# Gate and up products of a two-block network by Strassen's scheme, with the weight sums on GpSimd

## What is computed

```python
D_FF = 2816
def swiglu(h, w_gate, w_up, w_down):      # h: 512 x 1024, w_gate, w_up: 1024 x 2816, w_down: 2816 x 1024
    return (jax.nn.silu(h @ w_gate) * (h @ w_up)) @ w_down
```

## Time and profile before

| | |
|---|---|
| median of 3 runs | 3660.88 us (3645.41 to 3666.68) |
| profiled execution | 3647.48 us, span 3645.7 us |
| TensorE busy | 3278.3 us (90%) |
| VectorE, ScalarE, GpSimd busy | 1494.4, 1061.4, 171.7 us |
| granted TensorE clock, mean | 0.948 |
| one gate and up stage of an FFN | 238.6 us |

### The profile page before, as it was taken

One profiled execution on the slowest core, in us unless ns is written; L12 is line 12 of the kernel. 1 busy time (PEld: TensorE's weight loads), 2 busy tenths in 40 slices (PEclk: granted clock), 3 DMA queues, 4 the chain that ended last, 5 costly groups with the idle time before them and its releaser, 6 DMA issues. The chain is left out here.

```text
span 3645.7 us, 53714 instructions
## 1 busy us (share of the span) xinstructions
PE 3278.3 (90%) x23844; PEld 2475.4 (68%) x23844; DVE 1494.4 (41%) x2122; ACT 1061.4 (29%) x1666; POOL 171.7 (5%) x167
## 2 busy tenths in 40 slices
PE   6988778887998875999998799999999998799999
PEld 5856667764443333887786478878887886478877
DVE  3356665556121115333434553334333334553333
ACT  3226433321100002222323642223222323652222
POOL 0002222131000000000000000000000000000000
PEclk8999888997999997999999799999999999799999
DMA  6140000013799995222221032223332131032221
GB/s 235 58 159 1 3 4 3 34 64 136 317 408 422 421 421 201 93 93 93 74 106 58 1 104 93 93 93 99 102 100 93 70 110 58 1 104 93 93 93 41
DMA packets 173986, 441.04 MB, mean 121 GB/s; under 512 B 5954, under 2 KB 97852, under 8 KB 149180
## 3 DMA queue, kind: packets, MB, share of 16 engines
q1 hardware_dynamic: 173756, 437.61, 32.4%
HBM read 435.49 MB, written 2.10 MB: 120 GB/s over the span
## 5 line engine op out<-in xcount | busy, mean ns | idle before, releaser
L338 PE MATMUL banks<-mix_r,ring_r 128*128 128x512 f32 x1680 | 660.2, 393 | 0.0
L338 PE MATMUL banks<-mix_r,ffn_r 128*128 128x512 f32 x1568 | 622.4, 397 | 0.0
L338 PE MATMUL banks<-h_r,ffn_r 128*128 128x512 f32 x1568 | 610.2, 389 | 0.0
L295 DVE TENSOR_TENSOR ring_r<-ring,ffn_r 128x2048 fp32r<-128x2048 f32 (+1 forms) x166 | 354.9, 2138 | 220.6 <-ACT ffn_r L292 220.3
L292 ACT ACTIVATE ffn_r<-ring 128x2048 fp32r<-128x2048 f32 (+1 forms) x166 | 297.5, 1792 | 449.8 <-PE banks L338 440.5
L338 PEld LDWEIGHTS banks<-mix_r,ring_r 128*128 128x128 f32 x1680 | 315.4, 188 | 78.0
L338 PEld LDWEIGHTS banks<-h_r,ffn_r 128*128 128x128 f32 x1568 | 294.3, 188 | 68.5
L338 PEld LDWEIGHTS banks<-mix_r,ffn_r 128*128 128x128 f32 x1568 | 294.3, 188 | 62.2
L2261 PE MATMUL banks<-ring,arena 128*64 128x512 f32 x1120 | 261.6, 609 | 43.1 <-DMA ring<-in_exp_w_gate 16.8
L2887 PE MATMUL banks<-ring_r,ffn_r 128*128 128x512 f32 x704 | 279.3, 397 | 0.0
L2886 PE MATMUL banks<-ffn_r 128*128 128x512 f32 x640 | 250.7, 392 | 4.7 <-DVE arena L2837 4.7
(11 more groups left out here) (451 smaller groups left out, 5169.9 us busy)
## 6 DMA issues: line engine op xcount, KB each, us to landing
ring<-in_exp_w_gate SPq DMA_DIRECT2D x31, 2048.0 KB, 17.6
ring<-in_w_ffn_gate SPq DMA_DIRECT2D x44, 1024.0 KB, 5.4
ring<-in_w_ffn_up SPq DMA_DIRECT2D x44, 1024.0 KB, 8.0
ring<-in_exp_w_down SPq DMA_DIRECT2D x20, 2048.0 KB, 17.7
ring<-in_w_ffn_down SPq DMA_DIRECT2D x20, 2048.0 KB, 7.8
ring<-in_exp_w_up SPq DMA_DIRECT2D x19, 2048.0 KB, 14.8
ring<-in_w_in SPq DMA_DIRECT2D x17, 2048.0 KB, 8.2
arena<-in_exp_w_up SPq DMA_DIRECT2D x13, 2048.0 KB, 18.4
```

What stands on the lines that cost most here:

```text
L295: l.did(V.tensor_tensor(lo, x_, hi, ALU.subtract).then_inc(l.sem, 1), name, "lo", v)
L338: ins = TE.matmul(m[1](bank), m[2], m[3], start=m[4], stop=m[5])
```

## The change

For the first slab (feature tiles 0 and 1) of each FFN nothing changes in the mathematics. For the other ten slabs, each matrix (gate, up) is a unit v = 0 to 19 of its own, 1024 x 256. The product (weights transposed, 256 x 1024, by hT, 1024 x 512) is cut in quarters: the weights in A11, A12, A21, A22 (128 features by 512 of K), hT in B11, B12, B21, B22 (512 of K by 256 tokens), and computed by Strassen's scheme in Winograd's form with 7 products in place of 8. S1, S2, S3, S4 are sums of weight quarters, made on GpSimd; T1 to T4 are those of hT, made once for each FFN on VectorE and GpSimd. Each product is 12 matmuls of 256 columns (4 blocks of K, three for each), and some accumulate in the bank region of another; the remaining sums (V, U2, C12, C21, C22) are made on VectorE. The activation is now SiLU on the gate quarters and a product with the up quarters. The raw weights lie in four buffers of 1 MB (two ring slots); the other two ring slots hold the T's and half of the sums. The down weights use only the two ring slots of the raw weights, its high parts three buffers instead of two, and the fence ahead of the down stage is gone; instead there are single waits.

The diff, cut to its core (`load_raw`, `operand`, the first slab's four groups and the buffers' addresses are left out):

```diff
-                def ffn(l_, f_, early, behind, hooks=()):
+                def ffn(l_, f_, early, behind, hooks=None):
...
+                                me.wait_ge(*past(sx, "used", v - 4))
...
+                    def diff_dve(l, d):
+                        l.wait_ge(*past(sx, "B12"))
+                        if d == "T3":
+                            ins = V.tensor_tensor(by_tile(diff["T3"]), in_bank(1), b12, ALU.subtract)
+                        elif d == "T1":
+                            l.did(V.tensor_tensor(by_tile(diff["T1"]), b12, by_tile(B11[0]), ALU.subtract).then_inc(l.sem, 1))
+                            l.wait_ge(*l.own())
+                            ins = V.tensor_tensor(diff["T1"], diff["T1"], B11[1], ALU.subtract)
+                        else:
+                            l.wait_ge(*past(sx, "T1"))
+                            ins = V.tensor_tensor(by_tile(diff["T2"]), in_bank(1), by_tile(diff["T1"]), ALU.subtract)
+                        l.did(ins.then_inc(l.sem, 1), sx, d)
+
+                    def diff_pool(l):
+                        l.wait_ge(*past(sx, "T2"))
+                        l.did(G.tensor_tensor(diff["T4"], B21[0], diff["T2"], ALU.subtract).then_inc(l.sem, 1), sx, "T2_read")
+                        l.wait_ge(*l.own())
+                        l.did(G.tensor_tensor(diff["T4"], diff["T4"], B21[1], ALU.add).then_inc(l.sem, 1), sx, "T4")
...
+                    def sums_pool(l, v):
+                        l.wait_ge(*raw_full[v])
+                        if v >= 2:
+                            l.wait_ge(*past(sx, "used", v - 2))
+                        elif v == 1:
+                            l.wait_ge(*past(nm, "used", 1))
+                        s1, s2, s4 = (operand(v, s)[0] for s in ("S1", "S2", "S4"))
+                        l.did(G.tensor_tensor(s1, raw(v, "S3"), raw(v, "A22"), ALU.add).then_inc(l.sem, 1), sx, "S1", v)
+                        l.wait_ge(*l.own())
+                        l.did(G.tensor_tensor(s2, s1, raw(v, "A11"), ALU.subtract).then_inc(l.sem, 1), sx, "S2", v)
+                        l.did(G.tensor_tensor(raw(v, "S3"), raw(v, "A11"), raw(v, "S3"), ALU.subtract).then_inc(l.sem, 1), sx, "S3", v)
+                        l.wait_ge(*past(sx, "S2", v))
+                        l.did(G.tensor_tensor(s4, raw(v, "A12"), s2, ALU.subtract).then_inc(l.sem, 1), sx, "S4", v)
...
+                    SUM_AFTER = {"A11": "S3", "A12": "S4", "A22": "S1", "S1": "S2", "S2": "S4", "S3": "S3", "S4": "S4"}
+
+                    def lo_dve(l, v, name):
+                        if v >= NU:
+                            return
+                        l.wait_ge(*past(sx, "hi", v, name))
+                        l.wait_ge(*past(sx, SUM_AFTER[name], v))
+                        x_, lo, hi = operand(v, name)
+                        l.did(V.tensor_tensor(lo, x_, hi, ALU.subtract).then_inc(l.sem, 1), sx, "lo", v, name)
...
+                    FREE_BANK = {7: "P1c", 6: "P5c", 2: "V", 3: "U2", 4: "C11"}
+
+                    def s_pe(l):
+                        for v in range(NU):
+                            opened = set()
+                            for p in (1, 5, 7, 6, 2, 3, 4):
...
+                                l.wait_ge(*past(sx, "lo", v, name))
+                                if p in FREE_BANK:
+                                    l.wait_ge(*past(sx, FREE_BANK[p], v))
...
+                                for k in range(4):
+                                    TE.matmul(out_, a_hi[:, k, :], b_hi[:, k, :], start=(o not in opened), stop=False, skip_group_check=True)
+                                    opened.add(o)
+                                    TE.matmul(out_, a_hi[:, k, :], b_lo[:, k, :], start=False, stop=False, skip_group_check=True)
+                                    ins = TE.matmul(out_, a_lo[:, k, :], b_hi[:, k, :], start=False, stop=(k == 3), skip_group_check=True)
+                                l.did(ins.then_inc(l.sem, 1), sx, "P", p, v)
+                            l.name_last(sx, "used", v)
...
+                    def s_act(l):
...
+                        diff_hi(l, "T1")
+                        for v in range(NU):
+                            hi_act(l, v + 1, "A22")
+                            if v % 2:
+                                silu768(v - 1)
+                            l.wait_ge(*past(sx, "P", 1, v))
+                            if v:
+                                l.wait_ge(*past(sx, "C21", v - 1))
+                            l.did(S.activation(c1, place(v, 1), ACT.Copy).then_inc(l.sem, 1), sx, "P1c", v)
+                            hi_act(l, v + 1, "A11")
+                            hi_act(l, v + 1, "S1")
+                            l.wait_ge(*past(sx, "P", 5, v))
+                            l.did(S.activation(c5, place(v, 5), ACT.Copy).then_inc(l.sem, 1), sx, "P5c", v)
+                            hi_act(l, v + 1, "S2")
+                            hi_act(l, v + 1, "S3")
+                            hi_act(l, v + 1, "A12")
+                            if v % 2 == 0:
+                                l.wait_ge(*past(sx, "P", 2, v))
+                                l.did(S.activation(head256(v), place(v, 2), ACT.Silu).then_inc(l.sem, 1), sx, "C11", v)
+                            hi_act(l, v + 1, "S4")
...
+                    def s_dve(l):
+                        diff_lo(l, "T1")
+                        diff_lo(l, "T4")
+                        for v in range(NU):
+                            lo_dve(l, v, "A12")
+                            lo_dve(l, v, "S4")
+                            lo_dve(l, v + 1, "A22")
+                            lo_dve(l, v + 1, "S1")
+                            l.wait_ge(*past(sx, "P5c", v))
+                            l.wait_ge(*past(sx, "P", 7, v))
+                            l.did(V.tensor_tensor(c5, place(v, 7), c5, ALU.add).then_inc(l.sem, 1), sx, "V", v)
+                            lo_dve(l, v + 1, "A11")
+                            l.wait_ge(*past(sx, "P1c", v))
+                            l.wait_ge(*past(sx, "P", 6, v))
+                            l.did(V.tensor_tensor(c1, place(v, 6), c1, ALU.add).then_inc(l.sem, 1), sx, "U2", v)
+                            lo_dve(l, v + 1, "S3")
...
+                            lo_dve(l, v + 1, "S2")
+                            if v == NU - 1:
+                                split_first(l)
...
+                            l.did(V.tensor_tensor(c21, place(v, 4), c1, ALU.add).then_inc(l.sem, 1), sx, "C21", v)
+                            if v % 2:
+                                l.wait_ge(*past(sx, "silu768", v - 1))
+                                l.wait_ge(*l.own())
+                                l.did(V.tensor_tensor(tail768(v), t_, tail768(v), ALU.mult).then_inc(l.sem, 1), sx, "hid", v)
...
-                    stage(dn, pe=down_pe, act=split_down, dve=split_down)
+                    stage(dn, fence=False, pe=down_pe, act=split_down, dve=split_down)
```

More of the change, by code:

```diff
@@ L2804, in ffn @@
                     hid = free.take(NF, T)
[L2805 to L2813, removed]
+                    hid_r = parts_of("hid_r", hid_at, NF * T)
@@ new lines, in ffn, with parts @@
+                    hid_lo = hid_r(hid_at, NF, T)
+                    t_at = [free.at + i * 2048 for i in range(3)]
+                    free.take(3, 2048)
+                    c1, c5, c3 = free.take(256), free.take(256), free.take(768)
+                    assert free.at <= ARENA - D
+                    gt_at = mixT_at + KD * T
+                    two_r, tail_r = parts_of("two_r", gt_at, 2 * D), parts_of("tail_r", t_at[0], 3 * 2048)
+                    def parts(at_, *shape):
+                        return (ring_r if at_ < RING_WORDS else two_r if at_ < base.at else tail_r)(at_, *shape)
@@ L2814, in ffn @@
                     wg, wu, wd = (a["w_ffn_" + n + "_2"][l_, f_] for n in ("gate", "up", "down"))
                     src = lambda w, c: w.rearrange("(k p) n -> p k n", p=P)[:, :, c * 256:(c + 1) * 256]
+                    n0 = n_loads[0]
+                    C_, D_, A_, B_ = ((n0 + i) % RING for i in range(4))
+                    NU = NF - 2
                     gs, units = [], []
[L2817 to L2843, removed]
@@ new lines, in ffn, with raw @@
+                    load_raw(0)
+                    load_raw(1)
+                    yield nm, units[0], gs[0:2]
+                    for v in range(2, NU):
+                        load_raw(v)
+                    sums_at = (B_ * SLOT + 2048, t_at[0])
+                    his_at = (t_at[2], t_at[1])
+                    QUADS = {"A11": (0, 0), "A12": (0, 1), "S3": (1, 0), "A22": (1, 1)}
+                    def raw(v, name):
+                        i, j = QUADS[name]
+                        return region(raw_at[v % 4], KD, 256)[:, 4 * j:4 * j + 4, i * P:(i + 1) * P]
@@ new lines, in dve2, with act3, dve3 @@
+                    def dve2(l):
+                        lo_dve(l, 0, "S3")
+                        diff_lo(l, "T2")
```

(29 more changed lines are left out.)

161 lines of the change are left out of this document (153 added, 8 removed).

## The result

The changed kernel takes 3899.94 us (median of 4 runs, 3899.2 to 3905.97) against 3661.97 us before: a ratio of 1.065, interval 1.0621 to 1.0679. The forecast was 3762, its range ended at 3815. The sign and the waits are as forecast; another 138 us are not.

What follows compares the result with a forecast made beforehand. TensorE's matmuls were taken as the bound. Each FFN: 17.2 + 9 x 24.7 + 9.95 = 249.4 against 221.8, minus 0.2; four times +110 on 3647.5 gives 3757, leaned toward the median 3762 us; range 3600 to 3815.

Steps and rivals of the forecast that it cites:

- 1800:1840: Stretch of the earlier profile, TensorE idle 3.2 us in all at clock 1.00; cited for waits not costing the clock.
- the forecast's own waits: TensorE ahead of product 2, waiting for V: 1.97 us in odd units, 2.8 us in even ones.
- the clock falls too: Rival: new gaps lower the clock; a tenth of the stages at half clock adds 30 to 60 us; chance 0.12.
- Prices by distance: A matmul costs the distance to the next start: 0.2311 us with 512 columns, 0.1184 us with 256.
- a unit of 9.95: One weight slab of one matrix, 84 matmuls of 256 columns: 9.95 us on TensorE, against 11.09 before.
- 7 for 8: Seven products a unit in the gate and up stages: if TensorE alone decides, 80 x 1.14 = 91 us saved.
- Turns of one GpSimd and one VectorE operation: At the shared SBUF port, VectorE operations with two SBUF inputs alternate with GpSimd's; one turn of each takes 1.68 us.
- VectorE keeps the port: Rival: VectorE holds its turn while its queue is full, so TensorE bounds; 3561 us; chance 0.14.
- the term: Waits at product 2 in the units beside GpSimd, over the four FFNs: +172 us.
- The first unit's waits: Unit 0 of each FFN: product 2 waits for V(0), starting at about 29.9; the unit takes 17.2 us.
- The down stage: Start without the fence: a gap of 0.95 us instead of 1.17, 0.2 us gained in each, 1 in all.
- the ring's two slots: Down stage's weight loads fed from two slots: cost nothing, cover 9 us.

Runs made afterwards that it cites:

- experiment 6: GpSimd's sums replaced by memsets in the changed kernel, plus three, four, five or six VectorE operations ahead of V: 3698.75, 3745.05, 3858.83, 3990.66 us.
- after: The changed kernel as first written, against the kernel before: 3899.94 us, ratio 1.065.
- Experiment 2: Changed kernel with V and U2 moved earlier in VectorE's order, V ahead of three low parts: 3613.2 us in the repeat, ratio 0.9868 to the kernel before.
- Experiment 3: Changed kernel with the four weight sums made by VectorE instead of GpSimd from unit 1 on: 3640.93 us, ratio 0.9947 to the kernel before.
- 8: Changed kernel with V alone moved directly behind A12's low part, U2 left behind all the low parts: 3778.47 us in one run.

## Why the prediction was wrong

**What failed** is one sentence: "TensorE's waits of 2 to 3 us would not cost the clock by themselves: at 1800:1840, idle for 3.2 us in all, it kept 1.00". The clock cost 114.0 us, 77% of what the sum lacked (258.5 - 110 = 148.5), and the waits alone bring it on (experiment 6). The row was read as a sum where its parts decided. TensorE's waits of the kernel before in that stretch:

```profile
PE banks L334 <- DVE h_r L2627: 1.6, 1, 1.6
PE banks L378 <- DVE arena L2609: 1.3, 1, 1.3
PE banks L2552 <- DVE arena L2620: 0.2, 1, 0.2
```

None is above 1.6, a length that experiment 6 shows to be harmless even when it comes back in each unit; the forecast's own waits were 2 and 2.8. The row proves nothing of those. The rival *the clock falls too* was the right one and got 0.12, and its price was small: it let a tenth of the stages run at half clock. In after some 1200 matmuls at 0.213 are 255 of 1120 us, 23%, and each costs 0.09 us more.

**What held.** Prices by distance: 0.1184, a unit of 9.95, 7 for 8 worth 91.7 us. Turns of one GpSimd and one VectorE operation: the low part behind the 768 product starts 1.71 us before the next, forecast 1.68. Here too the trace agrees with the exclusion that the Trainium skill states (SBUF — State Buffer, section "Who interferes with whom"), and order of start alone doesn't explain it: VectorE, with its queue full, never had two turns together until GpSimd had ended (3641.31). The rival *VectorE keeps the port* needed just that. Waits of 1.88 and 2.73 against 1.97 and 2.8, at product 2, released by V, with the last unit free. The 11 us by which the term was low are the 0.23 us of each restart (16.6), less the shorter waits.

**Nearly the right sum, in another place.** The first unit's waits cost 9 us where 7.25 were forecast, but I had them at product 2, for V(0). TensorE waits 6.1 us on average at product 5 for the low part of T1 (L2931) and 2.15 us ahead of product 1; by then V is on time. The down stage gained 0.4 us of the 1 forecast: its gap is 1.07, I had 0.95.

**The 17 us outside the stages** were not in any term. 12 of them lie ahead of block 2 and in the token mixers, where the code is the same; block 2 begins anywhere between 1437.0 and 1468.8 us in the executions shown here, so I claim no cause for them. The down stages are another matter: they take 495.9 us or more in every changed kernel and 493.3 before. The forecast put the ring's two slots at no cost, and here are some 3 us that no run explains.

**The other experiments' numbers.** Experiment 2 came better than expected, since I had reckoned VectorE full with turns all through the unit; its own waits for the products let GpSimd through. Experiment 3 came 40 to 80 us above its forecast: I had counted VectorE's work but not where C11 stands in its queue, and at 189 of 214.5 us it is nearly full; the two were not tried apart. The waits of experiments 6 and 8 are other than expected too, which moved the points at which the clock was tried, not what they show.

## What to carry to other kernels

Seven products for eight are worth their full price in every unit in which TensorE is the only bound (9.95 us against 11.09): with V and U2 ahead of the low parts and the first unit put in order, the same arithmetic on the same engines takes 0.9825 of the time before (0.9783 to 0.9867), and as it was written 1.065. The first units, still 16.1 us, give some of the gain back. Put an operation that TensorE waits for ahead of those that share a port with GpSimd, not behind them. And price a wait of TensorE that comes back each dozen microseconds by its length and its neighbours', not by the stage's total: in these runs up to 1.6 us it costs itself and 0.23, from 2.2 us on the clock falls too and costs another 1.2 to 1.9 us for each on average.

## What the runs showed of the hardware

- The step in the clock: 1.61 us of wait in each unit of 11.8 leaves 0.5 us of slow matmuls in 72 units, 2.19 us in each of 12.4 or more makes them 88.9. A kernel between the two (1.40 and 1.95 in turn, 6.3 us) and after (1.88 and 2.73 in turn, slow behind the 1.88 as well) show that it is no single length.
- In the unit of after shown above the slower matmuls come behind the wait and not with it: the clock is 1.00 up to it, and the first starts 0.21 us apart come 0.8 us after TensorE resumes.
- At the lower level a matmul of 256 columns starts 0.213 us after the last, 1.8 times the 0.1184 of the upper level and not twice.
- GpSimd's memsets don't hold VectorE up at all (0.68 us beside ten of them in a row, where GpSimd's sums make it 1.7 to 1.8).
